# Two attention layers of a transformer stack: large projections in three fp32r passes instead of one fp32 pass, with the weight split, the modulation sums and the rotations rearranged

## The reference, cut to what matters

```python
def hybrid_layer(x, c, w_ada, b_ada, w_in, b_f, cmp_pe, cmp_w1, cmp_w2, w_out, ln_g, ln_b):
    shift, scale, gate = jnp.split(c @ w_ada + b_ada, 3, axis=-1)
    u = x * (1.0 + scale[:, None, :]) + shift[:, None, :]
    h = split_cols(u @ w_in)
    dq = rope(h["dsa_q"].reshape(B, S, DSA_HEADS, HEAD_DIM), pos)
    ...
    o_dsa = dsa_mixer(dq, dk, h["dsa_v"], iq, ik, iw)
    ...
    o_fox = fox_mixer(fq, fk, fv, logf)
    ...
    o_nsa = nsa_mixer(grp(nq), grp(nq_rot), kc, vc, ks, kvs("nsa_vs"), kw, kvs("nsa_vw"), gates)
    mix = jnp.concatenate([...], axis=-1)
    y = (mix * jax.nn.silu(h["gate"])) @ w_out
    return layer_norm(ALPHA * x + (1.0 + gate[:, None, :]) * y, ln_g, ln_b)
```

## Time and profile before

| what | value |
|---|---|
| timed runs | 2141.93 us median, 2141.18 to 2146.71 us (3 runs) |
| profiled execution | 2141.1 us of span, 0.8 us below the median; the page gives no other time for it |
| busy TensorE, VectorE, ScalarE, GpSimd | 2068.3, 1508.6, 1010.9, 50.8 us |
| first attention layer | 38 to 285 us |
| second attention layer | 285 to 525 us |
| mixer, dense stage, mixer | 525 to 1117 us |
| expert stage | 1117 to 2141 us |

### The profile page before, as it was taken

One profiled execution on the slowest core, in us unless ns is written; L12 is line 12 of the kernel. 1 busy time (PEld: TensorE's weight loads), 2 busy tenths in 40 slices (PEclk: granted clock), 3 DMA queues, 4 the chain that ended last, 5 costly groups with the idle time before them and its releaser, 6 DMA issues.

```text
span 2141.1 us, 26780 instructions
## 1 busy us (share of the span) xinstructions
PE 2068.3 (97%) x10468; PEld 1647.7 (77%) x10468; DVE 1508.6 (70%) x1833; ACT 1010.9 (47%) x1092; POOL 50.8 (2%) x56
## 2 busy tenths in 40 slices
PE   7999999999989999999988999999999999999996
PEld 4786577756876799888747888888888888888885
DVE  4565434554597545438858889888898889888887
ACT  1121312122223334313236777777777777777774
POOL 0000000000011000000200000000000000000000
PEclk9999999999999999999998999999999999999999
DMA  9844043611621365552138999999999999999991
GB/s 355 279 136 170 30 140 106 228 51 33 217 78 41 103 193 197 176 182 80 39 124 290 371 355 366 348 349 377 347 375 331 367 368 356 376 322 376 353 366 40
DMA packets 238750, 502.74 MB, mean 235 GB/s; under 512 B 11274, under 2 KB 53026, under 8 KB 238626
## 3 DMA queue, kind: packets, MB, share of 16 engines
q1 hardware_dynamic: 238626, 501.04, 65.6%
HBM read 499.96 MB, written 1.05 MB: 234 GB/s over the span
## 4 chain that ended last, share of the span: by engine, by line
PE 91%; DVE 7%; ACT 1%; issue 1%; DMA 0%; SPq 0%; DVEq 0%; ACTq 0%
PE bank L1549 14%; PE bank L1518 9%; PE bank L1520 9%; PE bank L1519 9%; PE bank L782 6%; PE bank L1221 6%; PE bank L1014 3%; PE bank L1089 3%; PE bank L790 3%; PE bank L1191 3%; PE bank L1197 3%; PE bank L1458 3%; PE bank L1429 2%; PE bank L1428 2%; PE bank L1427 2%; PE bank L1393 2%
## 5 line engine op out<-in xcount | busy, mean ns | idle before, releaser
L2766 DVE TENSOR_TENSOR ring_r<-ring,his 128x2048 fp32r<-128x2048 f32 x240 | 549.1, 2290 | 87.8 <-ACT his L1699 86.9
L1699 ACT ACTIVATE his<-ring 128x2048 fp32r<-128x2048 f32 x240 | 460.1, 1917 | 133.2 <-PE bank L1520 76.8
L1518 PE MATMUL bank<-his,xe_hi 128*128 128x512 f32 x896 | 353.7, 395 | 4.2 <-DVE ring_r L2766 4.2
L1520 PE MATMUL bank<-his,xe_lo 128*128 128x512 f32 x896 | 349.5, 390 | 0.0
L1519 PE MATMUL bank<-ring_r,xe_hi 128*128 128x512 f32 x704 | 274.2, 389 | 0.0
L2766 DVE TENSOR_TENSOR more_raw_r<-more_raw,his 128x2048 fp32r<-128x2048 f32 x96 | 220.0, 2291 | 28.7 <-ACT his L1699 28.2
L1699 ACT ACTIVATE his<-more_raw 128x2048 fp32r<-128x2048 f32 x96 | 184.1, 1918 | 54.8 <-PE bank L1549 29.3
L1518 PEld LDWEIGHTS bank<-his,xe_hi 128*128 128x128 f32 x896 | 168.3, 188 | 41.0 <-DVE ring_r L2766 5.4
L1520 PEld LDWEIGHTS bank<-his,xe_lo 128*128 128x128 f32 x896 | 168.2, 188 | 35.9
L1519 PEld LDWEIGHTS bank<-ring_r,xe_hi 128*128 128x128 f32 x704 | 132.2, 188 | 26.5
L1221 PE MATMUL bank<-uT,ring 128*128 128x256 f32 (+1 forms) x768 | 150.9, 359 | 0.0
(11 more groups left out here) (448 smaller groups left out, 3046.1 us busy)
## 6 DMA issues: line engine op xcount, KB each, us to landing
ring<-in_moe_w_gate_dram SPq DMA_DIRECT2D x96, 1024.0 KB, 5.4
ring<-in_moe_w_up_dram SPq DMA_DIRECT2D x80, 1024.0 KB, 5.8
ring<-in_moe_w_down_dram SPq DMA_DIRECT2D x64, 1024.0 KB, 5.4
more_raw<-in_moe_w_down_dram SPq DMA_DIRECT2D x48, 1024.0 KB, 5.3
ring<-in_w_in_dram SPq DMA_DIRECT2D x16, 2048.0 KB, 11.7
more_raw<-in_moe_w_up_dram SPq DMA_DIRECT2D x32, 1024.0 KB, 5.4
ring<-in_w_ada_dram SPq DMA_DIRECT2D x12, 2048.0 KB, 10.4
ring<-in_w_out_dram SPq DMA_DIRECT2D x8, 2048.0 KB, 9.7
```

What stands on the lines that cost most here:

```text
L1518: mm(bank[b][:, :], xe_hi[:, a, k, :], hi[:, kk, :], start=(k == 0), stop=False)
L1520: last = mm(bank[b][:, :], xe_lo[:, a, k, :], hi[:, kk, :], start=False, stop=(k == KD - 1))
L1699: return go(out, in_, ACT.Copy, scale=scale)
L2766: tt(piece_lo(s), piece_raw(s), piece_hi(s).bitcast(fp32), ALU.subtract).then_inc(S("lo_ready"), 1)
```

## The change

1. **Three passes.** In both attention layers 16 feature tiles (`iq0` to `nq2`), the 402 columns `nsa_vs` to `nsa_g` and the 390 columns `fox_v` and `fox_f` are split into high and low parts and multiplied in three fp32r matmuls each. `idx_k`, `idx_w`, `dsa_k`, `dsa_v`, the output gate and the output projection stay fp32. The weights are cut into 24 pieces per layer; the high part of a piece takes one of 5 places of 1,024 columns (`high`), the low part overwrites the raw weights in the ring. ScalarE makes the high parts (`weights_hi`), VectorE the low ones (`weights_lo`), each just ahead of use at written-out places. u is split too (`u_high`, `u_low`).
2. **Values and window keys.** `nsa_vs`, `nsa_kw`, `nsa_vw` and `nsa_g` become one stream of 402 columns per token tile; `window_keys` makes the keys once more in transposed form. The 18-column and 128-column matmuls of before go.
3. **Order.** The fox values and forget gate move to the front of the layer, right behind the indexer's key and weights; `ks` goes before `nq`; index scores 5 to 7 go behind the first `kc` tile.
4. **Modulation sums.** The 64 steps of VectorE are no longer eight in a row but one to four at a time (`ada_more`), many of them in the loop from group 5 on; the gate sums and `ada_gate` go to groups 18 and 20.
5. **Rotations.** VectorE also makes the cosine product; GpSimd has nothing left to do in the layers.
6. **Ring.** 4 slots instead of 5, each load with a slot written out by hand; behind the attention layers they are used in the turn 0, 2, 3, 1. The memory of the fifth slot and 1 K columns more hold the high parts, and in the expert stage two of the 14 places.
7. In the second half of the transposed mix VectorE instead of ScalarE copies out of PSUM; the gate projection's first half moves into the loop.

```diff
-W_IN_PARTS = [("idx_q", "idx_w"), ("dsa_q", "dsa_v"), ("fox_v", "fox_f"), ("fox_q", "fox_q"), ("fox_k", "fox_k"),
+W_IN_PARTS = [("fox_v", "fox_f"), ("idx_q", "idx_w"), ("dsa_q", "dsa_v"), ("fox_q", "fox_q"), ("fox_k", "fox_k"),
...
+SLOTS = 4
+HIGHS = 5
+HIGH = 1024
...
-GATE_PART_AT = {5: 1, 7: 2, 8: 3, 10: 4, 12: 5, 14: 6, 16: 7}
+GATE_PART_AT = {5: 0, 6: 1, 8: 2, 9: 3, 11: 4, 13: 5, 15: 6, 17: 7}
+ADA_GATE_AT = {18: 0, 20: 1}
+LAST_SCALE_AT = 8
+ADA_SUMS = [[(1, 0), (1, 1), (1, 2), (1, 3), (0, 4), (0, 5)], [(1, 4), (1, 5)]]
+SELECT_AT = {n: (n + 1,) for n in range(5, 15)}
...
             for k in range(KD):
-                    last = mm(b[0:n, to + tokens.start:to + tokens.stop], w[:, k, a:a + n], uT[:, k, tokens],
-                              start=(k == 0), stop=(k == KD - 1))
+                    mm(o, hi[:, k, a:a + n], uh[:, k, tokens], start=(k == 0), stop=False)
+                    mm(o, hi[:, k, a:a + n], ul[:, k, tokens], start=False, stop=False)
+                    last = mm(o, lo[:, k, a:a + n], uh[:, k, tokens], start=False, stop=(k == KD - 1))
...
+            def weights_hi(l, upto):
+                while split_at[0] <= piece_order[l, upto]:
...
+                    act.wait_ge(slot_loaded[slot_of[n]], loaded[ll, part])
...
+                    copy(high_part(ll, p), raw_part(ll, p)).then_inc(S("w_hi"), 1)
+                    split_at[0] += 1
...
                 if l == 0:
+                    weights_hi(0, "fv0")
...
                     for q in range(4):
                         copied(act, jobs[shift_scale_of(0, q)])
+                    scaled_pair(1)
+                    u_high_pair(0)
+                    u_high_pair(1)
+                    weights_hi(0, "fv1")
+                    scaled_pair(3)
...
+            def weights_lo(l, upto):
+                while split_at[0] <= piece_order[l, upto]:
+                    ll, p = list(piece_order)[split_at[0]]
+                    dve.wait_ge(S("w_hi"), split_at[0] + 1)
+                    tt(low_part(ll, p), raw_part(ll, p), high_part(ll, p).bitcast(fp32), ALU.subtract).then_inc(S("w_lo"), 1)
+                    split_at[0] += 1
...
-                    nc.gpsimd.tensor_tensor(rope_t2[0:r, n % 2, 0:tiles * T].rearrange("p (a t) -> p a t", a=tiles),
...
+                copied(dve, jobs[l, PROJECTED[name]])
+                tt(rope_t2[0:r, n % 2, 0:w].rearrange("p (a t) -> p a t", a=tiles), raw[name][0:r, :, :],
...
-                rope(l, "iq")
-                rope(l, "ik")
...
+                weights_lo(l, "fq0")
                 if l == 0:
-                    ada_sum(1, 3)
+                    ada_more(l, 4)
+                rope(l, "iq")
+                weights_lo(l, "fq1")
+                rope(l, "ik")
+                if l == 0:
+                    ada_more(l, 4)
+                rope(l, "dq")
+                weights_lo(l, "fk0")
+                rope(l, "dk")
...
+    add_in(0, "idx_q", 0)
+    add_in(0, "fox_v", 1)
+    add_in(0, "dsa_q", 2)
+    add_in(0, "fox_q", 3)
+    add_in(0, "fox_k", 1)
+    add_ada(1, 0, 0)
+    add_in(0, "nsa_kc", 2)
+    add_ada(1, 1, 0)
```

More of the change, by code:

```diff
@@ new lines, in build @@
+    for q in range(4):
+        add_ada(0, q, q)
+    add_in(0, "idx_q", 0)
[6 more added lines that the diff above has]
+    add_ada(1, 1, 0)
+    add_in(0, "nsa_q", 3)
+    add_in(0, "nsa_vs", 1)
+    add_ada(1, 2, 0)
+    add_cmp(0, 2)
+    add_ada(1, 3, 0)
+    add_gate(0, 0, 3)
+    add_ada(0, 4, 2)
+    add_gate(0, 1, 1)
+    add_ada(0, 5, 0)
+    add_out(0, 0, 3)
+    add_out(0, 1, 1)
@@ L408, in build @@
                 k = min(4, KF - 4 * n)
-                add_load(("ffn", 0, f"down{n}"), k, D,
+                add_load(("ffn", 0, f"down{n}"), next(turn), k, D,
                          A["ffn_w_down_2"][0][4 * n * P:(4 * n + k) * P, :].rearrange("(k p) n -> p k n", p=P))
+    moe_slots = [next(turn) for _ in range(SLOTS)]
     ctx = ExitStack()
@@ L472, in build @@
         vblk = sb("vblk", [NHC, NSA_HEADS, HD])
+        lows = ExitStack()
+        place[0] = lows
+        ul = sb("ul", [P, KD, T], fp32r)
+        lows.close()
+        place[0] = first
         sg = sb("sg", [P, NT, D])
@@ L917, in _ @@
+                    done(index_weight(1), j)
+                    split_tile(l, 1)
+                forget(l)
+                fox_values(l, 1)
+                feats(l, "iq", "iq0", "iq1")
+                feats(l, "dq", "dq0", "dq1")
                 if l == 0:
@@ L1144, in _ @@
                 done(compress(1), jobs[l, "ch"])
-                done(values(1), jobs[l, "vsw"])
-                ada_gate(1)
-                rotate(l, "ks")
-                j = jobs[l, "kwg"]
-                b = take(pe, j)
-                feat(b, l, "nsa_kw", 0, P, 0)
-                for i in range(NT):
-                    last = tok(b, l, "nsa_vs", at("nsa_g"), 18, i, T + 18 * i)
-                done(last, j)
+                rotate(l, "nq2")
+                window_keys(l)
+                values(1)
                 j = jobs[l, "ckv"]
@@ L1768, in _ @@
[L1768 to L1779 removed]
+                weights_hi(l, "fk0")
@@ L2438, in _, with blocks @@
                 b = filled(dve, j)
-                for v in range(2):
+                def blocks(v):
                     for g in range(NSA_GROUPS):
@@ L2506, in _ @@
                         mixed(n - 2)
-                    if n in SELECT_AT:
-                        select(SELECT_AT[n])
+                    for step in SELECT_AT.get(n, ()):
+                        select(step)
+                    ada_more(l, 2 if l == 0 and n < 9 else 1)
+                    if l == 0 and n == LAST_SCALE_AT:
+                        shift_scale(1, 3)
+                    if n - 1 in ADA_GATE_AT:
+                        dve.wait_ge(S("gate_bias"), 16 * (l + 1))
+                        gate(ADA_GATE_AT[n - 1])
                 for i in range(NT):
```

703 lines of the change are left out of this document (457 added, 246 removed).

## The result

The changed kernel takes 2132.24 us (median of 4 runs, 2130.33 to 2133.63), the kernel before 2142.57 on the same chip: the medians lie 10.3 us apart, and the ratio taken over the runs is 0.9945, interval 0.9931 to 0.9959, which is 11.8 us less. Forecast were 31 less, 2111 within 2101 to 2126: the direction held, the number and the range did not. Measured once more on another chip the ratio was 0.9948 (e9).

The account below looks back on a forecast made before the run. TensorE, busy 97% of the span, was taken to bound the kernel. 34.6 saved plus 4.1 clock less 9.2 losses gave 29.5 us, a walked schedule 32; 31 was taken, so 2111 us, range 2101 to 2126.

Parts of the forecast that it names:

- The pitch of 0.12 us and the tile of 2.88: Feature tiles: 24 fp32r matmuls of 256 columns, 0.12 us apart, take 2.88 us instead of 3.55, gaining 0.67 each.
- `fox_v` landed at 37.55: Start of the first layer: these weights, 1.6 MB more to load, were to land at about 37.6 us.
- The indexer's key: Start of the first layer: the key ends at 43.7 us instead of 41.5 without the wait, a loss of 2.2.
- Behind the layers nothing changed: Mixers, dense stage and experts: instructions unchanged, only load starts shift, everything keeps its length; ring cost 0.
- VectorE did not become the bound: Attention layers: VectorE rises from 112 to about 146 us of some 187, 78%, and does not become the bound.
- The stops, 9.2 us forecast: Both layers' losses where lists are late: start 2.2, iq1/dq1 1, sums 1, fox softmax 3.5, loop 1.5.
- splits too late: Rival, weight pieces: VectorE or ScalarE misses TensorE at most pieces; half of 48 late costs 14 us, 2125; chance 0.15.
- The clock: Gate projection half: without the 18-column matmuls it runs at full clock, gaining 2.4 + 1.7 = 4.1 us.
- as they are on TensorE's list in either place, they cost the same: Both layers: partition sums, rotations, index scores, gate and output projection are only moved and cost TensorE no more.
- TensorE's work saved: Both layers: tiles 11.4, forget gate 0.7, fox values 2.4, other values 2.8, or 17.3 us a layer, 34.6 in all.
- Sums in the first layer: First layer's modulation sums: ada0 lands some 10 us behind iq, VectorE waits 2 to 3; at most 1 us lost.
- The forecast itself: Whole kernel: 31 us less, 2111 us; chance 0.75 of landing between 2103 and 2120.

Follow-up runs that it names:

- e9: The changed kernel once more, unedited, on another chip: 2133.42 us, ratio 0.9948 to the kernel before.
- e11: Changed kernel with rows loaded later, sum steps, third shift_scale and gate part 0 moved, two loads exchanged, banks changed for index and fox scores: 2108.26 us, ratio 0.9827.
- e6: Changed kernel with gate part 0 moved ahead of scores(5), where TensorE waited for vblk: 2126.47 us, ratio 0.9906.
- e1: Changed kernel with the three broadcast rows (1.5 MB) loaded behind nsa_vs instead of ahead of ada0: 2127.58 us, ratio 0.9911.
- e10: Changed kernel with one TensorE wait added behind the second layer's dsa queries, until ScalarE has copied them: 2135.90 us, ratio 0.9958.
- e13: e11 with four of the six heads left out of the compressed group's scores: 2111.49 us, ratio 0.9849.
- e14: e11 with 14 of the 16 matmuls of each compression left out: 2102.42 us, ratio 0.9805.
- e12: e11 with the index scores in four pairs: 2107.27 us, ratio 0.9823.
- e15: e12 with gate part 0 split, half ahead of scores(5) and half between scores(5) and scores(6): 2108.61 us, ratio 0.983.
- e7: Changed kernel with the first five index scores of each layer in pairs, score 4 joining 5 to 7: 2136.10 us, ratio 0.9956.
- e3: Changed kernel with 48 of 64 modulation sum steps left out, landings and waits kept: 2121.93 us, ratio 0.9885.
- e4: Changed kernel with the rotations' cosine products back on GpSimd, as in the kernel before: 2130.57 us, ratio 0.9922.

## Why the prediction was wrong

**Right.** The pitch of 0.12 us and the tile of 2.88. `fox_v` landed at 37.55 (forecast 37.6). The indexer's key ended at 43.1 (43.7). Behind the layers nothing changed by more than the scatter. VectorE did not become the bound (e11). The stops, 9.2 us forecast, were 9.0 to 9.4 in the ledger, though not where I put them: TensorE waited 1.4 us in all for low parts, and that behind sum steps, so the rival *splits too late* is out, while 1.3 us at the relu stood in no term. In size, the 20 us missing at the second output projection are the clock and TensorE's own work, the first and second step below; the third says where the largest of the stops came from.

**First failed step: "The clock".** I counted 4.1 us gained. The ledger has 6.4 to 8.8 lost, so 10 to 13 of the 20 us missing. The dip behind the 18-column matmuls was read rightly from the earlier trace rows, but without them the gate half still took 6.36 and 5.33 us against the earlier trace rows's 6.06 and 5.33. Ahead of it there is still few-column work, and now a stop too; with the stop gone a dip remained (e6), so this part of the cause is argued. Behind each new stop I had priced the stop alone. What the runs put in its place: a stop of 0.5 to 1.5 us in a stretch of short matmuls is mostly followed by 3 to 7 us at half clock. At scores(0) 19 of the 22 layers traced with the stop of 0.67 us (the changed kernel and e1 to e10) had the dip; the 10 layers traced there without a stop (before, e11, e13, e14, the second of e12 and of e15) had none. The first layers of e12 and e15 stop for 0.5 us a little later, and one of the two has the dip. Two stops of 1.0 us ahead of 402-column matmuls (e14, at 140 and 144 us) had none. The tiles behind have less than the whole time to lose: at 0.21 for 0.12, 24 passes cost 2.2 us more.

The Trainium skill's "TensorE: Matmul & The Clock Gate" (A second HAM failure mode: psum-queue depth-cycling) describes short idle moments between groups of matmuls that make the clock swing. The traces agree at scores(0), and e10 (0.7 us, clock 1.00) shows that idle moments alone don't do it.

**Second: "as they are on TensorE's list in either place, they cost the same".** They don't once the tiles around them are fp32r. The ledger gives 26 to 27 us of TensorE's work saved, not 34.6. Each return from an fp32 operation shows as a first matmul of 0.31 for 0.12, and an index score alone costs what a pair did in the kernel before. Six groups instead of four, and five of them single scores, cost 0.94 us for each group that e7 took away, 2.8 a layer, 5.6 in both. The other 2 to 3 us are argued only: rotations and scores between tiles have the same 0.31 behind them.

**Third: "Sums in the first layer", at most 1 us.** It was 2.7 us of stop and 3.4 of clock. I let `ada0` land 10 us behind `iq` and VectorE wait 2 to 3 us for it; it waited 8.5. It was issued at 65.58, with 1.5 MB of broadcast rows (issued from 60.08 to 61.18, in no term of mine) still on their way, and took 11.7 us; without them it took 8.3 (e1). And I did not ask how long VectorE then takes to work off its list: four sum steps, a rotation, a low part, a second rotation, four more sum steps, which `shift_scale` waits for, a third rotation and the next low part, which a tile waits for (e1, e3).

The forecast itself was a sum for a kernel without these. e11, with every split, sum and rotation as in the change, but with order, banks and loads mended, begins the second output projection 27.3 us earlier than the kernel before, and e12 32.0 (464.2 against 496.3), where the prediction had 31. That e11's median of 2108.26 lies so near 2111 is partly luck: on its chip the kernel before takes 2145.49, and the part behind the layers came out at its short end.

One number ahead of the prediction is wrong: `u @ w_in` has 4,032 columns, not 3,986. No sum uses it.

## What to carry to other kernels

Price a stop of TensorE twice, with its own length and with a few microseconds at 1.2 GHz, wherever short or few-column matmuls stand near; a stop of 0.7 us with its dip costs more than the 0.67 us that one feature tile gains. When tiles change type, group what stays fp32 between them. And where one engine's in-order list holds both work that others wait for and work that waits for a load, walk the loader's list too, every transfer in it.

## What was not expected of the hardware

- The same program with the same stop of 0.67 us had clock 0.61 or 1.00 in the next 4 us (e9 against the first profile), and the unchanged part behind the layers took 1640 to 1645 us in different executions.
- A dip can stand behind few-column matmuls without a stop (e6, 6.44 us for 3.63), and goes when few-column work 15 us earlier is left out (e14).
- An isolated fp32 index score among fp32r tiles took 0.64 us, two took 0.65, and two took 0.65 among fp32 tiles as well.
- A copy of VectorE beside a GpSimd product took 0.78 us for 0.20 (e4).
